# Sum of experts in a two-layer mixture-of-experts network: order of the row transfers and of TensorE's terms

## What is computed

```python
def moe_ffn(t, ...):
    scores = jax.nn.sigmoid(tf @ router_w)
    _, idx = lax.top_k(scores + router_bias, TOP_K)
    gate = jnp.take_along_axis(scores, idx, axis=1)
    gate = ROUTED_SCALE * gate / jnp.sum(gate, -1, keepdims=True)
    ...
    for e, g in the 8 experts and gates of tok:
        acc[tok] += (silu(tf[tok] @ w1[e]) * (tf[tok] @ w3[e])) @ w2[e] * g
    shared = (jax.nn.silu(tf @ sw1) * (tf @ sw3)) @ sw2
    return acc[:n_tok] + shared

h = layer_norm(DEEPNORM_ALPHA * h + mod[5] * f, ln_w[l, 1], ln_b[l, 1])
```

## Time and profile before

| what | us |
|---|---|
| median of three executions | 2463.77 (2463.47 to 2467.29) |
| the profiled execution, its own time | 2451.74 |
| its span from the first to the last instruction | 2449.9 |
| changed stage in layer 0, from SyncE's first issue to VectorE's last instruction | 1419.62 to 1488.39 |
| changed stage in layer 1, likewise | 2401.17 to 2444.69 |

### The profile page before, as it was taken

How to read it: one execution, slowest core, us unless ns; L and a number is a source line. 1 busy time by engine, 2 the same in 40 slices (tenths; PEclk the granted TensorE clock), 3 DMA queues, 4 the chain that set the end, 5 groups by cost and what they waited for, 6 DMA issues and landing times. The chain is left out here.

```text
span 2449.9 us, 31472 instructions
## 1 busy us (share of the span) xinstructions
PE 1977.4 (81%) x10528; PEld 1017.6 (42%) x10529; DVE 854.2 (35%) x1752; ACT 236.7 (10%) x517; POOL 680.4 (28%) x967
## 2 busy tenths in 40 slices
PE   3795759935788899899999976959778988787795
PEld 0342523323446454455555433324455544344442
DVE  0004720057545333233333344554343322222224
ACT  1102110122002000000000011001110000000001
POOL 0000000021101566456666400000005654444440
PEclk8895679977897999999999987979879999999998
DMA  9400047300206699999899575121238999999944
GB/s 378 181 1 1 0 176 291 121 1 1 91 0 279 229 410 411 414 408 393 348 409 393 218 309 216 69 107 65 90 130 358 415 420 422 422 422 420 419 194 189
DMA packets 99974, 601.65 MB, mean 246 GB/s; under 512 B 23200, under 2 KB 23435, under 8 KB 40444
## 3 DMA queue, kind: packets, MB, share of 16 engines
q1 hardware_dynamic: 66012, 516.78, 51.5%
q0 software_dynamic: 33888, 83.86, 9.2%
HBM read 590.50 MB, written 51.92 MB: 262 GB/s over the span
## 5 line engine op out<-in xcount | busy, mean ns | idle before, releaser
L1609 PE MATMUL bank<-moe_w,blk_xT 128*64 128x256 f32 x5632 | 679.4, 396 | 2.7 <-DVE blk_xT L1685 2.7
L1609 PEld LDWEIGHTS bank<-moe_w,blk_xT 128*64 128x64 f32 x5632 | 404.4, 142 | 220.1 <-issue 32.2
L1620 PE MATMUL bank<-moe_w,xt 128*64 128x512 f32 x1408 | 332.1, 592 | 1.5 <-DVE xt L1697 1.5
L1536 POOL DMA_INDIRECT ada_rows<-v_tokens,blk_gidx x264 | 272.5, 1032 | 140.2 <-issue 135.1
L451 PE MATMUL bank<-w_in_ring,xt 128*128 128x512 f32 x544 | 241.7, 604 | 13.0 <-DMA w_in_ring<-in_odd_w_in 10.2
L1685 DVE STREAM_TRANSPOSE blk_xT<-ada_rows 128x512 f32<-128x512 f32 x132 | 94.0, 712 | 450.8 <-PE bank L1609 427.1
L1552 POOL DMA_INDIRECT y_rows<-xt,blk_sidx x176 | 179.9, 1022 | 94.6 <-issue 48.4
L1704 DVE COPY xt<-bank 128x512 f32<-128x512 f32 x176 | 121.8, 692 | 149.3 <-PE bank L1620 149.3
L451 PEld LDWEIGHTS bank<-w_in_ring,xt 128*128 128x128 f32 x544 | 104.3, 194 | 148.1 <-issue 137.5
L1620 PEld LDWEIGHTS bank<-moe_w,xt 128*64 128x64 f32 x1408 | 100.9, 137 | 127.5 <-issue 100.5
L1668 ACT ACTIVATE xt<-bank 128x128 f32<-128x128 f32 x174 | 48.3, 278 | 1046.7 <-PE bank L1609 1046.7
(11 more groups left out here) (386 smaller groups left out, 1746.4 us busy)
## 6 DMA issues: line engine op xcount, KB each, us to landing
moe_w<-in_experts SPq DMA_DIRECT2D x128, 3072.0 KB, 31.0
ada_ring<-in_ada_w SPq DMA_DIRECT2D x12, 2048.0 KB, 17.2
w_out<-in_ada_w POOLq DMA_DIRECT2D x12, 2048.0 KB, 8.8
moe_w<-y_rows SPq DMA_DIRECT2D x24, 1024.0 KB, 20.5
w_in_ring<-in_even_w_in SPq DMA_DIRECT2D x8, 2048.0 KB, 12.6
w_in_ring<-in_odd_w_in SPq DMA_DIRECT2D x7, 2048.0 KB, 19.2
ada_rows<-v_tokens,blk_gidx POOLq DMA_INDIRECT x264
w_out<-in_even_w_out SPq DMA_DIRECT2D x1, 4096.0 KB, 12.3
```

The costliest lines, as they stand in the source:

```text
L1536: pool.indirect_dma_start(came[q][:, u], None, v_quarters, bass.IndirectOffsetOnAxis(ap=gidx[q][:, u:u + 1], axis=0), bounds_check=4 * n_t ...
L1609: last = nc.tensor.matmul(g.bank[1][64 * h:64 * h + 64, 0:HID], xT[:, k], w[:, s, (2 * k + h) * HID:(2 * k + h + 1) * HID], start=k == 0, ...
L1620: last = nc.tensor.matmul(g.bank[3][64 * h:64 * h + 64, :], hT[:, 64 * m:64 * m + 64], w[:, s, at:at + 512], start=m == 0, stop=m == 1)
```

## The change

The row transfers of a tile are issued in the order of pairs 2, 3, 0, 1 (`ORDER`), so that rows 4 to 7 come ahead of rows 0 to 3. The load of `sh_down` moves from the head of the queue to behind the four transfers of tile 0, and `ln` stands behind it. On TensorE a tile begins with row 4, then rows 0 to 3 (`BY_PE_ORDER`), and the shared expert's eight records stand at the end of the tile instead of its start. VectorE waits for a new semaphore, `summed`, that the last of them raises. ScalarE makes the diagonals in TensorE's new order. The conditions under which SyncE may reuse a place of the ring follow the new orders.

```diff
@@ -1093,11 +1093,13 @@
 
     nc = g.nc
     nt = len(tiles)
-    (ln_loaded, step, rooted, normed, diag_made, rows_used, rows_added) = (new_sem(g, x) for x in (
-        "ln_loaded", "ln_step", "ln_root", "ln_normed", "diag_made", "y_rows_used", "y_rows_added"))
+    (ln_loaded, step, rooted, normed, diag_made, rows_used, rows_added, summed) = (new_sem(g, x) for x in (
+        "ln_loaded", "ln_step", "ln_root", "ln_normed", "diag_made", "y_rows_used", "y_rows_added", "y_summed"))
     BY_PE = 5
     BY_DVE = TOPK - BY_PE
     PAIRS = TOPK // 2
+    ORDER = (2, 3, 0, 1)
+    BY_PE_ORDER = (4, 0, 1, 2, 3)
     RING = 13
     fetched = [new_sem(g, f"y_fetched{s}") for s in range(RING)]
     rows = y_dram.rearrange("(n p j k) d -> n j p k d", p=P, j=PAIRS, k=2)
@@ -1113,40 +1115,42 @@
         marks = {}
 
         def piece(n, k):
-            u = n * PAIRS + k // 2
+            u = n * PAIRS + ORDER.index(k // 2)
             return u % RING, 16 * (u // RING + 1)
 
         with nc.Block() as block:
             @block.sync
             def _(sp):
-                load_expert(sp, sh_down, g.dram["experts"][l * (EXPERTS + 1), W13 // PIECE:]).then_inc(sh_down_loaded, 16)
                 for u in range(nt * PAIRS):
                     if u >= RING:
-                        n, j = (u - RING) // PAIRS, (u - RING) % PAIRS
-                        by_pe = min(2 * j + 2, BY_PE)
-                        sp.wait_ge(rows_used, n * BY_PE + by_pe)
-                        if 2 * j + 2 > BY_PE:
+                        n, j = (u - RING) // PAIRS, ORDER[(u - RING) % PAIRS]
+                        if j != 3:
+                            sp.wait_ge(rows_used, n * BY_PE + (1 if j == 2 else 2 * j + 3))
+                        if j >= 2:
                             sp.wait_ge(rows_added, n * BY_DVE + 2 * j + 2 - BY_PE)
-                    sp.dma_start(ring[:, u % RING], rows[u // PAIRS, u % PAIRS]).then_inc(fetched[u % RING], 16)
-                    if u == 0:
+                    sp.dma_start(ring[:, u % RING], rows[u // PAIRS, ORDER[u % PAIRS]]).then_inc(fetched[u % RING], 16)
+                    if u == PAIRS - 1:
+                        load_expert(sp, sh_down, g.dram["experts"][l * (EXPERTS + 1), W13 // PIECE:]).then_inc(sh_down_loaded, 16)
                         sp.dma_start(ln, g.dram["ln_rows"][l, 1]).then_inc(ln_loaded, 16)
 
             @block.tensor
             def _(pe):
-                pe.wait_ge(sh_down_loaded, 16)
                 for n in range(nt):
+                    for m, k in enumerate(BY_PE_ORDER):
+                        at, count = piece(n, k)
+                        pe.wait_ge(fetched[at], count)
+                        pe.wait_ge(diag_made, n * BY_PE + m + 1)
+                        for half in range(2):
+                            last = nc.tensor.matmul(g.bank[2 * n + half][:], diag[:, n * BY_PE + k], ring[:, at, k % 2, half * 512:(half + 1) * 512],
+                                                    start=m == 0, stop=False)
+                        last.then_inc(rows_used, 1)
+                    if n == 0:
+                        pe.wait_ge(sh_down_loaded, 16)
                     for m in range(2):
                         for half in range(2):
-                            nc.tensor.matmul(g.bank[2 * n + half][:], r["sh_hidden"][m][:, n * P:(n + 1) * P],
-                                             sh_down[:, m * D + half * 512:m * D + (half + 1) * 512], start=m == 0, stop=False)
-                    for k in range(BY_PE):
-                        at, count = piece(n, k)
-                        pe.wait_ge(fetched[at], count)
-                        pe.wait_ge(diag_made, n * BY_PE + k + 1)
-                        for half in range(2):
-                            last = nc.tensor.matmul(g.bank[2 * n + half][:], diag[:, n * BY_PE + k], ring[:, at, k % 2, half * 512:(half + 1) * 512],
-                                                    start=False, stop=k == BY_PE - 1)
-                        last.then_inc(rows_used, 1)
+                            last = nc.tensor.matmul(g.bank[2 * n + half][:], r["sh_hidden"][m][:, n * P:(n + 1) * P],
+                                                    sh_down[:, m * D + half * 512:m * D + (half + 1) * 512], start=False, stop=m == 1)
+                    last.then_inc(summed, 1)
 
             @block.vector
             def _(dve):
@@ -1164,7 +1168,7 @@
                         else:
                             nc.vector.scalar_tensor_tensor(zz, row, gate, zz, ALU.mult, ALU.add).then_inc(rows_added, 1)
                         dve.wait_ge(rows_added, n * BY_DVE + k - BY_PE + 1)
-                    dve.wait_ge(rows_used, (n + 1) * BY_PE)
+                    dve.wait_ge(summed, n + 1)
                     for half in range(2):
                         cols = slice(half * 512, (half + 1) * 512)
                         link(nc.vector.tensor_tensor(zz[:, cols], zz[:, cols], g.bank[2 * n + half][:], ALU.add))
@@ -1200,7 +1204,7 @@
             @block.scalar
             def _(act):
                 for n in range(nt):
-                    for k in range(BY_PE):
+                    for k in BY_PE_ORDER:
                         nc.scalar.activation(diag[:, n * BY_PE + k], g.ident, ACT.Copy, scale=r["gate"][:, n, k:k + 1]).then_inc(diag_made, 1)
                 for n in range(nt):
                     act.wait_ge(step, marks["var", n])
```

## The result

The changed kernel takes 2473.14 us, the median of 16 runs (2458.83 to 2480.08), against 2463.62 us for the kernel before in 16 runs beside it. The ratio is 1.0041, with a 95% interval of 1.0025 to 1.0057: slower by 10 us, between 6 and 14. The prediction was 2474.9 us.

The account below looks back on a forecast made before the run. The prediction took layer 1's stage as bound by the DMA queue, and TensorE and VectorE as nearly level in layer 0, just behind the transfers. 2463.77 + 4.0 + 5.4 + 1.7 gave 2474.9 us, range 2469 to 2480.

Parts of the forecast that it names:

- VectorE's first rows come earlier: Layer 0's stage: VectorE starts at 1424.46 instead of 1434.99, 10.5 us earlier, gaining nothing because it waits for `summed`.
- Bank read of tile 0, layer 0: Layer 0's first tile: read at 1438.6, or 1440.3 to 1443.2 if TensorE does not keep up, against 1440.20; all absorbed.
- What bounded layer 1 before: Layer 1's stage before the change: bound by the DMA queue, ten 1 MB transfers at 429 GB/s, 2.74 us of VectorE behind.
- First term, +4.0 us: Layer 0, tile 1's bank read: 24 TensorE records behind the ninth transfer, 1455.4 instead of 1451.43, +4.0 us.
- Second term, +5.4 us: Layer 1's last bank read: 24 records behind the ninth transfer, 2437.5 instead of 2432.09, +5.4 us.
- Third term, +1.7 us: Layer 1, tile 1: TensorE idles 1.3 to 3.2 us before the ninth landing, then one cold clock restart, +1.7 us.
- The rival with restarts in both layers: Both layers' stages: a cold clock restart in each, +12.8 to +14.8 us, about 2477.6 us; chance 0.18.
- Costs at nothing: Both stages: ScalarE's new order, fewer semaphore increments and SyncE's waits for places cost nothing; uncovered, each under 1 us.
- The total: Whole kernel: 4.0 + 5.4 + 1.7 = +11.1 us, giving a median of 2474.9 us.

Follow-up runs that it names:

- experiment 1: Changed kernel, but with the shared expert first on TensorE again in every tile after the first; stages 71.72 us (layer 0) and 46.68 us (layer 1).
- experiment 7: Kernel before, with VectorE's last-tile reciprocal and scale ahead of the previous tile's closing multiplications; stages 67.79 us (layer 0) and 43.45 us (layer 1).
- Experiment 3: Changed kernel, with the norm's rows loaded behind tile 1's four transfers instead of before them; stages 71.97 us (layer 0) and 46.80 us (layer 1).
- experiment 2: Changed kernel, plus two unused matmuls of constants in TensorE's pause in layer 1's second tile; stages 72.67 us (layer 0) and 49.30 us (layer 1).
- experiments 4: Changed kernel, with the sh_down load back at the queue's head and its matmuls first in every tile; stages 69.39 us (layer 0) and 45.54 us (layer 1).
- experiment 8: Kernel before, with last-tile scale ahead, norm's rows loaded later, and row 4 given to VectorE in some tiles; median 2457.85 us, ratio 0.9978.
- experiment 6: Changed kernel, with only the load of the shared expert's weights back at the queue's head; stages 72.81 us (layer 0) and 49.26 us (layer 1).

## Why the prediction was right, step by step

- **VectorE's first rows come earlier, and this gains nothing.** Right. It starts 4.9 us into the stage, where the first transfer lands, and then waits 12.19 and 12.00 us for L1151.
- **Bank read of tile 0, layer 0.** The forecast was 1438.6, or 1440.3 to 1443.2 if TensorE is late and cold, which is 20.7 to 23.6 us into the stage; it was 22.58. It was absorbed, as said. That it takes no part is true only where TensorE still has to wait for tile 1's ninth transfer: in experiment 1, where that pause is gone, the same late tile 0 is what bounds both stages. The prediction named the delay and gave it no price, since it was hidden behind a larger one.
- **What bounded layer 1 before.** The prediction named the transfers alone. They and TensorE were nearly level: by the earlier trace rows TensorE's last record ends at 2423.16 + 8.75 = 2431.91, 0.2 us ahead of the bank read at 2432.09. In experiment 7 VectorE waited 1.15 us for TensorE at that place. The sum does not hang on this, since it counts TensorE's records from the ninth landing.
- **First term, +4.0 us.** The ninth landing, forecast at 25.3 us into the stage, came at 25.1, and 24 records at full clock put the second read at 35.79. Measured +4.00. Experiment 3 took the pause away and found 0.8 us.
- **Second term, +5.4 us.** The ninth landing, forecast at 25.8 us, came at 25.9. Less the restart, layer 1 is 7.38 - 1.70 = 5.7 us longer, 0.3 more than the sum.
- **Third term, +1.7 us, one restart in layer 1.** The pause was forecast at 1.3 to 3.2 us and was 2.34. Measured 1.70 by comparing 8.83 with 7.13 us, and again by experiment 2, which kept the clock up and was 1.6 us shorter. The size was taken from the blocks stage, where a pause of 2.35 us had cost 1.7. The rival with restarts in both layers did not come about in tile 1, where it would have counted: layer 0's pause there was 0.93 us. The clock did fall in layer 0 too, behind tile 0's 1.86 us, where nothing waited for it. That tile 1's pause was short in layer 0 is in part luck, since it rests on how late tile 0 ends, and tile 0's burst of 16 records took 7.13 us in some executions and 8.65 to 9.26 in others. The Trainium skill, page "TensorE: Matmul & The Clock Gate", section "HAM oscillation — how this bites in real kernels", describes a kernel whose bursts are parted by waits for DMA of 3 to 5 us and start cold every time. This case's trace agrees that such a wait can cost the clock, and shows it for shorter ones, 1.86, 2.34 and 2.35 us; behind tile 1's pauses of 0.93 to 1.39 us the clock was at full.
- **Costs at nothing.** Right: the changed kernel's profile has no wait for a diagonal, and SyncE's waits for places are on no chain.
- **The total.** +11.1 forecast, +11.4 in the stages, +9.5 between the medians. I had kept the 12 us between the profiled execution and the median of before as an offset; experiments put it down to scatter ahead of these stages, in which that one execution was at the low end. Single executions scatter over some 20 us, so that the medians came within 2 us of 2474.9 shows less than the two stages do, and is in part luck.

The split of the loss, by experiments 4 and 1: in layer 0 the row order alone costs 0.6 us, and the shared expert's place with the later load the other 3.4; in layer 1 it is 2.0 and 5.4, of which 1.7 is the clock. The parts overlap, so other orders of undoing them give other shares.

## What to carry to other kernels

When a queue of transfers is the pace, count what stands behind the last landings on each engine, and put the work that needs no late data ahead of them, in the time an engine waits anyway. In these two stages an earlier start for one engine was worth nothing, as its partner's sum came last: 10.5 us of earlier start bought a 12 us wait. Of two engines that share a sum, try to take rows from the one whose records run unbroken to the end; experiment 8 did so and gained, together with two other edits.

## What the runs showed of the hardware

- The clock did not fall in the pause but after it: in layer 1 it was at full for 2.3 us of idle time and 0.4 us of work, then at 0.50 for 2.9 us (tile 1 of the changed kernel).
- Making data come later went with a shorter stage: with every row of tile 0 one transfer later, TensorE's pause in layer 1 fell from 2.34 to 1.37 us, the clock stayed at full, and the stage was 1.6 us shorter. Pauses of 1.86 and 2.34 us were followed by the low clock; tile 1's pauses of 0.93, 1.17, 1.20, 1.37 and 1.39 us were not. These are one execution each, so no limit between them is shown.
- Two matmuls whose result nobody reads, placed in a pause, went with a stage 1.6 us shorter and the clock at full behind the pause.
- What the clock does in the first tile after an idle stretch is not settled by what TensorE did in the stage. In layer 1 of the changed kernel it had 4 records of 3.78 us, a pause of 1.12 us, and 16 records of 8.67 us at a low clock that had not risen yet. In experiment 3 it was 3.73, 1.22 and 7.13 us, with the same start 4.9 us into the stage; in experiment 6 it was 3.78, 1.12 and 7.13 us. What tells these apart stays open, and it moves the end of tile 0 by 1.5 us.
